# Dropping the identity product of a refinement step: the residual made in two passes of VectorE

## The reference, cut to what matters

```python
lmat = jnp.where(strict, jnp.einsum('nbhid,nbhjd->nbhij', kb, k) * decay, 0.0)
tmat = lmat + jnp.eye(DN_CHUNK, dtype=F32)
rhs = jnp.concatenate([v * beta[..., None], kb * jnp.exp(gc)[..., None]], axis=-1)
sol = lax.linalg.triangular_solve(tmat, rhs, left_side=True, lower=True, unit_diagonal=True)
```

## Time and profile before

| | value |
|---|---|
| median of three runs | 2881.23 us |
| the profiled execution's own time | 2878.12 us |
| its span | 2876.3 us, 58157 instructions |
| busy, share of the span | PE 92%, ACT 43%, POOL 45%, DVE 42% |
| mean granted clock of TensorE | 0.964 |
| `refine_f` identity, L845 | 64 instructions, 468 ns each |
| `refine_f` products, L848 | 512 records, 274 ns each |
| `refine_r`, L1858 | 64 instructions, 687 ns each |
| stretch of the 16 refinements | 1180.4 to 2632.1 us from the span's start |

### The profile page before, as it was taken

One profiled execution on the slowest core, in us unless ns is written; L12 is line 12 of the kernel. 1 busy time (PEld: TensorE's weight loads), 2 busy tenths in 40 slices (PEclk: granted clock), 3 DMA queues, 4 the chain that ended last, 5 costly groups with the idle time before them and its releaser, 6 DMA issues.

```text
span 2876.3 us, 58157 instructions
## 1 busy us (share of the span) xinstructions
PE 2650.1 (92%) x24892; PEld 2223.1 (77%) x24892; DVE 1219.5 (42%) x2427; ACT 1233.4 (43%) x2210; POOL 1287.2 (45%) x780
## 2 busy tenths in 40 slices
PE   4699999999999665999999999999999999997898
PEld 0277777777778454888888888888888888886897
DVE  0212222222310322565565555655655566554323
ACT  2422333333322324465456545654565456443333
POOL 2032333333245524544554555455545554551353
PEclk8899999999999877999999999999999999998999
DMA  6835444455442202213222322232222222214554
GB/s 277 330 108 185 186 174 174 183 190 190 161 176 88 73 30 91 74 61 104 89 76 67 104 82 82 68 101 85 78 71 97 89 74 75 97 53 147 183 184 132
DMA packets 98897, 351.54 MB, mean 122 GB/s; under 512 B 10833, under 2 KB 15313, under 8 KB 96210
## 3 DMA queue, kind: packets, MB, share of 16 engines
q1 hardware_dynamic: 98642, 347.82, 34.3%
HBM read 335.59 MB, written 12.19 MB: 121 GB/s over the span
## 4 chain that ended last, share of the span: by engine, by line
PE 72%; POOL 12%; issue 6%; DVE 3%; DMA 3%; ACT 3%; SPq 0%; POOLq 0%; ACTq 0%; DVEq 0%
PE bank L522 8%; PE bank L524 7%; PE bank L523 7%; PE bank L684 4%; PE bank L686 4%; PE bank L685 4%; POOL wl L385 3%; PE bank L790 3%; PE bank L498 3%; POOL scratch L2059 2%; DMA raw<-w_ada 2%; PE bank L724 2%; PE bank L808 2%; PE bank L726 2%; PE bank L725 2%
## 5 line engine op out<-in xcount | busy, mean ns | idle before, releaser
L385 POOL TENSOR_TENSOR wl<-raw,wh 128x1024 fp32r<-128x1024 f32 x210 | 500.3, 2386 | 722.3 <-ACT wh L380 722.3
L380 ACT ACTIVATE wh<-raw 128x1024 fp32r<-128x1024 f32 x226 | 238.7, 1059 | 548.5 <-PE bank L686 258.4
L684 PE MATMUL bank<-hh,wh 128*128 128x512 f32 (+1 forms) x1040 | 410.6, 395 | 49.7 <-POOL wl L385 24.8
L686 PE MATMUL bank<-hh,wl 128*128 128x512 f32 (+1 forms) x1040 | 387.4, 372 | 0.9 <-issue 0.9
L685 PE MATMUL bank<-hl,wh 128*128 128x512 f32 (+1 forms) x1040 | 385.8, 371 | 1.3 <-issue 1.3
L684 PEld LDWEIGHTS bank<-hh,wh 128*128 128x128 f32 x1040 | 201.7, 194 | 86.1 <-POOL wl L385 25.9
L522 PE MATMUL bank<-hh,wh 128*128 128x512 f32 x640 | 256.8, 401 | 11.8 <-POOL wl L328 11.8
L328 POOL TENSOR_TENSOR wl<-raw,wh 128x1024 fp32r<-128x1024 f32 x56 | 136.7, 2446 | 254.7 <-ACT wh L323 254.7
L524 PE MATMUL bank<-hh,wl 128*128 128x512 f32 x640 | 250.4, 391 | 0.0
L523 PE MATMUL bank<-hl,wh 128*128 128x512 f32 x640 | 250.2, 391 | 0.0
L686 PEld LDWEIGHTS bank<-hh,wl 128*128 128x128 f32 x1040 | 201.3, 194 | 35.9 <-issue 1.7
(11 more groups left out here) (277 smaller groups left out, 5995.6 us busy)
## 6 DMA issues: line engine op xcount, KB each, us to landing
raw<-w_in SPq DMA_DIRECT2D x258, 512.0 KB, 3.5
raw<-w_ada SPq DMA_DIRECT2D x124, 512.0 KB, 6.5
raw<-w_out SPq DMA_DIRECT2D x84, 512.0 KB, 3.8
scratch<-w_ada SPq DMA_DIRECT2D x68, 512.0 KB, 6.3
scratch<-keep_g SPq DMA_DIRECT2D x16, 1024.0 KB, 6.0
scratch<-w_in SPq DMA_DIRECT2D x24, 512.0 KB, 7.0
scratch<-xT SPq DMA_DIRECT2D x2, 4096.0 KB, 12.8
keep_y<-scratch SPq DMA_DIRECT2D x30, 256.0 KB, 2.4
```

The lines of the kernel that those rows point to most:

```text
L380: eng.activation(buffers(s)[0], raw[:, s % RAW, :], ACT.Copy).then_inc(sem("rear_hi"), 1)
L385: eng.tensor_tensor(buffers(s)[1], raw[:, s % RAW, :], buffers(s)[0].bitcast(F32), ALU.subtract)\
L684: pe.matmul(ps, w[:, k * P:(k + 1) * P], hhv[:, kk, t0:t1], start=first and k == k0, stop=False)
L686: done = pe.matmul(ps, r[:, k * P:(k + 1) * P], hhv[:, kk, t0:t1], start=False, stop=last and k == k1 - 1)
```

## The change

TensorE's identity product is dropped, and with it `identr`, ScalarE's copy that made it and the wait on that. The bank now holds L D alone. VectorE makes the residual in two instructions for each `c`: the first reads the bank and `DT[c]` and writes -(bank) - `DT` as fp32 into half of the room of `DU`; a wait on its own semaphore follows (`ch.link`); the second adds the identity and writes `ZT[c]`. VectorE waits in addition on `dt_ready`, and at c = 0 on `d5_ready` (TensorE and ScalarE are done with `DU`). GpSimd's `first_inverse(h)` waits in addition on the `r_ready` of all four tiles of head h - 1.

```diff
-                    pe.matmul(pb[2 + c % 2][:, :], identr, DT[c], start=True, stop=False)
                     for u in range(4):
                         us = slice(u * P, (u + 1) * P)
                         done = pe.matmul(pb[2 + c % 2][:, us], CT(i, c)[:, us], DT[c][:, us].bitcast(F32),
-                                         start=False, stop=(u == 3))
+                                         start=True, stop=True)
...
-            pe.wait_ge(sem("identr_ready"), 1)
...
-            act.activation(identr, ident, ACT.Copy).then_inc(sem("identr_ready"), 1)
...
             def refine_r(i):
                 for c in range(NT):
                     dve.wait_ge(sem("f_made"), 4 * i + c + 1)
-                    dve.tensor_tensor(u4(ZT[c]), over4(ident), u4(pb[2 + c % 2][:, :]), ALU.subtract)\
+                    dve.wait_ge(sem("dt_ready"), 8 * i + 4 + c + 1)
+                    if c == 0:
+                        dve.wait_ge(sem("d5_ready"), 2 * (i + 1))
+                    room = DUall[:, (c % 2) * T:(c % 2 + 1) * T]
+                    ch.link(dve.scalar_tensor_tensor(out=room, in0=pb[2 + c % 2][:, :], scalar=-1.0,
+                                                     in1=DT[c].bitcast(F32), op0=ALU.mult, op1=ALU.subtract))
+                    dve.tensor_tensor(u4(ZT[c]), over4(ident), u4(room), ALU.add)\
                        .then_inc(sem("r_ready"), 1)
...
                 if h:
                     pool.wait_ge(sem("base_made"), 10 * h)
+                    pool.wait_ge(sem("r_ready"), 4 * h)
```

More of the change, by code:

```diff
@@ L209, in build @@
         invp = cut(NT)
-        identr = cut(P, F32R)
         CTb = [cut(NT * T), cut(NT * T)]
@@ L233, in build @@
         ZC = SR[0].rearrange("p (m n) -> p m n", n=B)
-        DU = cut(NT * 4 * 2 * B).rearrange("p (m s n) -> p m s n", s=2, n=B)
+        DUall = cut(NT * 4 * 2 * B)
+        DU = DUall.rearrange("p (m s n) -> p m s n", s=2, n=B)
         RB, VK, VO, UT = SR[3], VN[0], {2: VN[1], 3: VN[2]}, VN[3]
```

## The result

The change makes the kernel slower: 2908.97 us in the median of four runs (2904.7 to 2913.12) against 2882.09 (four runs, 2880.4 to 2884.49), 26.9 us more. The ratio is 1.0093, with a 95% interval of 1.0074 to 1.0111, which is 21 to 32 us. The forecast was 22.4 us more. The profiled execution took 2906.36 us, its span is 2904.5 us.

The account below looks back on a forecast made before the run. The prediction took GpSimd's string, started by VectorE's residuals and read_kq, to be what is late in each head; 15 x 1.28 + 3.19 = 22.4 us on 2881.23 gave 2903.6 us, range 2890 to 2917.

Parts of the forecast that it names:

- The handoff through `read_kq` and GpSimd: In each head GpSimd, started by read_kq after the residuals, is late; TensorE waits 0.57 us for it, 8.6 us together.
- The passes and their order: Four tiles' refinement, head 7: first passes 0.69 us, second passes held beside GpSimd; last residual ends 1865.09, before 1863.81.
- The term per head: The last residual, read_kq and GpSimd's string come 1.28 us later, all of it added to each of 15 heads.
- TensorE's own delay: TensorE reaches z_eighth some 0.5 us later in each head; its wait there grows from 0.57 to about 1.3 us.
- The rule that two such engines exclude each other for whole instructions: Rival for VectorE's SBUF-only passes beside GpSimd: last residual 1.63 us later per head, 3.34 in the last, 2909.0 us; chance 0.10.
- The last head: The third tile's second pass is held by a GpSimd split, making the last residual 3.19 us later; 1.10 if it misses.
- The sum: Whole kernel: 15 x 1.28 + 3.19 = 22.4 us more, 2903.6 us for the median.
- The rival of the clock: Longer TensorE waits bring the lower clock; another stretch like the last head's 21 us costs some 10 us: 2914; chance 0.05.
- The rival that TensorE keeps its saving: The refinement's tiles don't wait for VectorE: 64 x 0.29 = 18.6 us less, 2862.6 us; chance 0.04.

Follow-up runs that it names:

- kq_before: The kernel before the change, with make_kq and read_kq moved ahead of the refinement: 2870.49 us, ratio 0.9948 to 0.9976.
- kq_after: The changed kernel with make_kq and read_kq moved ahead of the refinement: 2896.77 us, ratio 1.0039 to 1.0069 against the kernel before.
- early_bank: The changed kernel, TensorE's third and fourth products waiting only until VectorE's first pass has read the bank: 2903.8 us (one run).
- psum_second: The changed kernel, its second pass reading the bank in place of the room of DU, DT left out of the residual: 2903.18 us.
- split_after: The changed kernel, GpSimd's first split of the last phase held until the last head's four residuals are done: 2903.68 us.
- one_pass: The kernel before with the identity product dropped, one VectorE pass per tile, and refine_p doubling DM to put the identity's share back: 2874.09 us.
- kq kernels: Kernels with make_kq and read_kq moved ahead of the refinement, made from the kernel before, the changed kernel and variants: medians 2862.88 to 2896.77 us.
- keep_identity: The changed kernel with the identity product put back, DT counted twice in the residual: 2918.65 us (one run).

## Why the prediction was right, point by point

- *The handoff through `read_kq` and GpSimd.* Right: all 15 heads are longer from A to Z by the same 1.12 us, and kq_before shows the handoff to be what was late before the change. After it the handoff carries a part only: kq_after loses as much a head without it, by more collisions, and free of collisions the handoff is worth 0.96 - 0.43 = 0.53 us of a head.
- *The passes and their order.* Right to 0.02 us. The four tiles' last residual ends 6.73 us after A (2167.84 - 2161.11); the steps gave 6.71. The first pass took the lower bound, 0.69 us; L2036's 1.42 us was put at 1.46, the stretched pass ends at 2165.11, 4.00 after A (4.03 was worked out).
- *The term per head*, 1.28 us: too large by 0.16. `attention` started 1.20 us after the last residual before and 1.01 after it now. Before, the first instruction of `read_kq` began at 1863.91, 0.10 us behind the residual, where it now begins 0.08 us ahead of the residual's end, so that it had been waiting for `make_kq`, not for VectorE; that little slack swallowed a part of the delay. 16.8 us in place of 19.2.
- *TensorE's own delay*: 0.5 us was given, 0.57 measured (5.93 against 5.36 us from A to the next L684). The wait at L724 was to grow to 1.3 us (20 in all) and grew to 0.88 (13.1 in all): some of it had moved ahead. L684 behind L889 now starts 1.03 us after it (2178.51) and not 0.67, held by an earlier split of GpSimd (early_bank shows that wait). TensorE comes to L724 0.81 us later than it did, and waits 0.32 longer there: the 1.12.
- *The rule that two such engines exclude each other for whole instructions* (the Trainium skill, SBUF — State Buffer, Who interferes with whom) is right in who collides: psum_second shows that one operand in PSUM is enough to be free of it. In size the traces went with L1597: the ends are 0.54 us behind GpSimd's, also in the last head (2656.37, against 2655.83), and not 0.69. GpSimd's next was longer by 0.38 us (1.42 against 1.04), not by a whole pass.
- *The last head*: the collision came as worked out, last residual 8.59 us after A (8.61 given, 5.42 before), 3.17 us later (3.19 given). But A to the projection grew by 5.9. The other 2.7 us were not in the sum. The clock is likely in them: from A to the projection it was at 0.50 for 27.3 us, before for 20.5, which at half the clock costs 3.4 us at most (an estimate). Where no pass collides there (split_after, psum_second) it was at 0.50 for 23.9 us, and the last residual 1.2 us later than before goes with a stretch 3.1 longer. What the clock cost in each wasn't taken apart.
- *What was missed*: 6.4 us from Z to A, for which the prediction had no term. Of these, 2.5 us are idle time of TensorE; waits put down to issue grew by 2.2 (11.0 us against 8.8). The other 3.9 us are longer busy time, and they go with the lower clock, 23.9 us in place of 10.2. Most of that lies in the stretch that leads into the last head: 17.1 us at 0.50 in place of 6.8. In head 8 TensorE had waited 2.05 us until 2032.65, and the clock fell at 2033.54, for 3.41 us; in head 10 it fell as a wait of 1.73 us ended. Issue waits of 1.54, 2.43 and 1.88 us in three other heads brought no fall, so that the waits as the cause of the falls are not shown.
- *The sum.* The steps that the prediction had, as measured, give 16.8 + 3.2 = 20.0, against 22.4; with 6.4 from Z to A and 2.7 in the last head it is 29.1, and the start, 1.45 shorter, and the end, 0.6 longer, make it the 28.2 of the span. That the forecast of the time is off by only 4.5 us is in part luck: a term per head too large by 2.4 us in all stood against 9.1 us that no step had.
- *The rival of the clock* came in small part: from Z to A and in the last head together TensorE was at 0.50 for 20.5 us more, but in pieces, and no single new stretch of 21 us.

The rival that TensorE keeps its saving failed: one_pass shows what dropping the product is worth when VectorE isn't charged for it, 0.66 us a head. The second pass takes that back and 1.12 more: it costs 1.78 (25.80 against 24.02).

What stays open: why the issue waits come where they do, and why the clock falls behind some of them only. Of the kernels with as many products as before, three had 1076.8 to 1077.5 us from Z to A and kq_before 1081 (with 0.86 a head for the moved `make_kq` taken off); those with fewer had 1083 to 1089 (the kq kernels likewise corrected). That is one profiled execution of each, so that chance isn't ruled out.

## What to carry to other kernels

Work taken off the engine with the largest busy share is worth what the wait behind it allows: here four products of 0.29 us each became four passes of 0.73 us on an engine that was 42% busy, yet its work stood in the one handoff that set the head, and beside GpSimd's. Look for algebra that removes the term from both engines, as one_pass does, and move work that others wait for (make_kq) ahead of work that only its own engine needs. Before adding a VectorE pass with both operands in SBUF, read what GpSimd does beside it.

## What the runs showed of the hardware

- A VectorE pass with both operands in SBUF (L1861) that started with 0.26 us or more of a GpSimd instruction still to run ended 0.54 to 0.55 us behind it: 0.81 us beside L2036, 2.66 us beside a split, in place of 0.69, and so in all 16 such passes of the changed kernel and all 61 of kq_after. With 0.11 us or less left (15 passes of the changed kernel) it kept its 0.69. The same pass with one operand in PSUM: 0.69 at most in 64.
- Which of them goes first turns on a quarter of a microsecond (0.69 against 1.51 us for the same pass in the changed kernel and in keep_identity).
- 64 products fewer of 24892 on TensorE went with 6.4 us more in the stretches between the refinements: 2.5 us of idle time and 3.9 us of longer busy time, with 23.9 us at a granted clock of 0.50 in place of 10.2. Putting back 64 products of two columns went with 1077.2 us in place of 1083.2 and with 10.2 us at 0.50 (one profiled execution of each).
